# Fifth modulation vector taken out of the attention heads and put ahead of them; all modulation vectors on four column groups of 32

## What is computed

```python
m = silu(cvec) @ w_mod[l] + b_mod[l]               # 1024 x 6144, for c_ctx and for c
sh1, sc1, g1, sh2, sc2, g2 = m.reshape(6, 1024)
h = rms_norm(x, n1) * (1 + sc1) + sh1
q, k, v, u = split(h @ w_in)                       # 8 query heads, 2 KV heads of 64; u is 2 x 512
attn = attention(norm_rope(q), norm_rope(k), v)    # latent tokens also see 128 cached keys
conv = silu(layer_norm(depthwise_conv31(glu(u))))
x = x + g1 * (concat(attn, conv) @ w_out)
h2 = rms_norm(x, n2) * (1 + sc2) + sh2
x = x + g2 * moe(h2)                               # 16 experts, best group of 4, top 2 in it
```

## Time and profile before

| | us |
|---|---|
| median of 3 runs | 1130.35 |
| the runs | 1130.08, 1130.35, 1140.29 |
| the profiled execution, its own time | 1134.84 |
| its span from first to last instruction | 1133.0 |
| PE busy in it | 1003.9 (89%) |
| DVE busy | 393.6 (35%) |
| ACT busy | 152.3 (13%) |
| POOL busy | 116.3 (10%) |

### The profile page before, as it was taken

How to read it: one execution, slowest core, us unless ns; L and a number is a source line. 1 busy time by engine, 2 the same in 40 slices (tenths; PEclk the granted TensorE clock), 3 DMA queues, 4 the chain that set the end, 5 groups by cost and what they waited for, 6 DMA issues and landing times. The chain is left out here.

```text
span 1133.0 us, 11425 instructions
## 1 busy us (share of the span) xinstructions
PE 1003.9 (89%) x4328; PEld 471.3 (42%) x4328; DVE 393.6 (35%) x857; ACT 152.3 (13%) x357; POOL 116.3 (10%) x176
## 2 busy tenths in 40 slices
PE   4799999999799998899899989999788888987993
PEld 1555544545233333333366534555433333333331
DVE  0159954334411111111035996434511111111106
ACT  1100144220000000000020014422000000000001
POOL 0100400501000000000111020050100000000001
PEclk9899989998899999999899999999689899999897
DMA  9926991259999996999980375235966999999814
GB/s 341 354 117 238 291 366 70 95 189 360 419 404 423 425 372 273 413 422 424 360 306 24 149 277 215 75 115 195 371 237 240 417 422 425 424 423 422 353 28 167
DMA packets 64406, 329.83 MB, mean 291 GB/s; under 512 B 6992, under 2 KB 9680, under 8 KB 47924
## 3 DMA queue, kind: packets, MB, share of 16 engines
q1 hardware_dynamic: 44224, 277.89, 61.2%
q0 software_dynamic: 8496, 28.68, 6.9%
q10 hardware_dynamic: 11588, 21.95, 5.9%
HBM read 306.67 MB, written 21.82 MB: 290 GB/s over the span
## 5 line engine op out<-in xcount | busy, mean ns | idle before, releaser
L1746 PE MATMUL ps<-big 128*64 128x512 f32 x1024 | 245.5, 631 | 29.0 <-DMA big<-in_w_up_dram 11.8
L1762 PE MATMUL ps<-big,scr 128*64 128x512 f32 x624 | 151.0, 623 | 5.3 <-DVE scr L1399 4.3
L1441 PE MATMUL ps<-big 128*128 128x384 f32 (+2 forms) x448 | 147.9, 492 | 5.2 <-ACT big L777 5.2
L1746 PEld LDWEIGHTS ps<-big 128*64 128x64 f32 x1024 | 81.7, 145 | 168.1 <-issue 157.1
L1102 DVE SCALAR_TENSOR_TENSOR scr<-scr,convw 128x384 f32<-128x384 f32 x240 | 134.0, 611 | 2.3
L1410 DVE TENSOR_TENSOR scr<-ps,scr 128x256 f32<-128x256 f32 x32 | 13.6, 425 | 315.5 <-ACT scr L932 315.5
L1441 PEld LDWEIGHTS ps<-big 128*128 128x128 f32 x448 | 86.0, 193 | 64.7 <-issue 24.6
L1457 PE MATMUL ps<-big,cs_rep 128*64 128x512 f32 x320 | 80.8, 656 | 14.0 <-DMA big<-in_w_mod_dram 14.0
L1762 PEld LDWEIGHTS ps<-big,scr 128*64 128x64 f32 x624 | 51.2, 143 | 91.1 <-issue 89.0
L1662 PE MATMUL ps<-big 128*128 128x512 f32 x192 | 84.4, 594 | 1.4 <-ACT big L817 1.4
L1746 PE MATMUL ps<-big,scr 128*64 128x512 f32 x224 | 51.3, 612 | 5.9 <-DVE scr L1388 5.9
(11 more groups left out here) (220 smaller groups left out, 819.7 us busy)
## 6 DMA issues: line engine op xcount, KB each, us to landing
big<-in_w_gate_dram SPq DMA_DIRECT2D x32, 2048.0 KB, 15.8
big<-in_w_up_dram SPq DMA_DIRECT2D x32, 2048.0 KB, 19.7
big<-in_w_down_dram SPq DMA_DIRECT2D x32, 2048.0 KB, 16.7
big<-in_w_mod_dram SPq DMA_DIRECT2D x23, 2048.0 KB, 15.5
big<-in_w_in_dram SPq DMA_DIRECT2D x6, 2048.0 KB, 26.8
expert_rows<-scr ACTq DMA_DIRECT2D x74, 128.0 KB, 8.2
big<-in_w_out_dram SPq DMA_DIRECT2D x4, 2048.0 KB, 15.6
expert_rows<-x ACTq DMA_DIRECT2D x1, 6912.0 KB, 42.0
```

Source lines behind the costliest of these rows:

```text
L1441: mm = pe.matmul(out, stationary(k), moving(k), start=(k == 0), stop=(k == n - 1))
L1746: mm = pe.matmul(ps[b * TT:(b + 1) * TT, bank, :].rearrange("p (m n) -> p m n", m=2), tokens(k), w[:, :, k, b * HF:(b + 1) * HF], start=(k ...
L1762: mm = pe.matmul(ps[b * TT:(b + 1) * TT, bank, :], src[:, k % 2 * P + k // 2 * TT:k % 2 * P + (k // 2 + 1) * TT], w[:, k, b * SEG:(b + 1) ...
```

## The change

All vectors, the fifth too, are computed on four lanes of 256 outputs, on column groups of 32: a k-step is four matmuls of 256 columns (eight records), `columns` has 32 matmuls for 16, `lane_in` and `lane_out` issue four DMAs for two. `head_fill` is gone. Vector 4 runs as a whole on PE after the third tile's transposes and the end of vector 3, ahead of the scores of head 0, into PSUM bank 2; DVE takes it right after vector 3, ahead of `score_max` of head 0, in two instructions of 256 columns each, and the transposes of head 0 wait for that take. Its bias and the norm weight come in by `lane_in` (four DMAs each for one), together with vector 3's; its store is four DMAs for one.

```diff
-LANES = 2
+LANES = 4
-TAKES = [0, 1, 2, 3, 8, 9, 5]
+TAKES = [0, 1, 2, 3, 4, 5]
-    return {3: 0, 8: 0, 9: 0, 5: 3}[j]
+    return {3: 0, 4: 2, 5: 3}[j]
-HEAD_FILL = [(8 + hd // 4, hd % 4 * (KD // 4), (hd % 4 + 1) * (KD // 4)) for hd in range(HEADS)]
...
                 lane_in(pool, rowB, b_mod[l:l + 1, 3 * D:4 * D], rowB_in)
-                pool.dma_start(rowS, b_mod[l:l + 1, 4 * D:5 * D].broadcast_to([2, D])).then_inc(rowB_in, 16)
+                lane_in(pool, rowS, b_mod[l:l + 1, 4 * D:5 * D], rowB_in)
+                lane_in(pool, gainB, norm2_g[l:l + 1, :], rowB_in)
...
-                pool.wait_ge(slot_used[slot_of(("in", l, 3))], uses(("in", l, 3)))
-                pool.dma_start(gainB, norm2_g[l:l + 1, :].broadcast_to([2, D])).then_inc(gain_in, 16)
                 pool.wait_ge(mod_done, l + 1)
                 lane_out(pool, mod_dram[:, 3 * D:4 * D], rowB, modB_st)
-                pool.dma_start(mod_dram[:, 4 * D:5 * D], rowS).then_inc(modB_st, 16)
+                lane_out(pool, mod_dram[:, 4 * D:5 * D], rowS, modB_st)
...
-                    v.tensor_copy(rowA[:, c * LW:(c + 1) * LW], ps[:, bank, :]).then_inc(mod_taken, 1)
+                    v.tensor_copy(rowA[:, c * LW:(c + 1) * LW], ps[:, bank, 0:LW]).then_inc(mod_taken, 1)
...
+                row = (rowC, rowB, rowS, rowG)[c - 2]
+                v.tensor_tensor(row, ps[:, bank, 0:LW], row, ALU.add).then_inc(mod_taken, 1)
+                if c == 4:
                     dve.wait_ge(mod_taken, taken_at(l, c))
+                    v.scalar_tensor_tensor(row, row, 1.0, gainB, ALU.add, ALU.mult).then_inc(mod_done, 1)
...
                 mod_take(l, 3)
+                mod_take(l, 4)
...
-                    if HEAD_FILL[hd][2] == KD:
-                        mod_take(l, HEAD_FILL[hd][0])
...
-                            mm = pe.matmul(ps[lane * LP:(lane + 1) * LP, mod_bank(l, j), :], cs_rep[:, k, :],
+                            mm = pe.matmul(ps[lane * LP:(lane + 1) * LP, mod_bank(l, j), 0:LW], cs_rep[:, k, :],
                                            w[:, lane * LW:(lane + 1) * LW], start=(k == 0), stop=(k == KD - 1))
...
+                vector(l, 4)
                 pe.wait_ge(qkT_ready, l * 4 + 4)
                 for t in range(TILES):
                     scores(0, t)
...
                         if hd == 0 and t == 0:
-                            pe.wait_ge(mod_taken, taken_at(l, 3))
+                            pe.wait_ge(mod_taken, taken_at(l, 4))
...
-                    head_fill(l, hd)
...
-                    if n == 0:
-                        pe.wait_ge(mod_taken, taken_at(l, 9))
```

More of the change, by code:

```diff
@@ L288, in build @@
         zT = cut(CM * CONV_W).rearrange("p (m n) -> p m n", m=CM)
-        assert o >= 5120 + 3 * LW
+        assert o >= 6656
         qk_sq = scr[:, TILES * 640 + 2 * 640:2 * TILES * 640 + 2 * 640].rearrange("p (t n) -> p t n", t=TILES)
@@ L293, in build @@
         ck = cut(KVW)
-        sg = rowC = cut(CH)
+        sg = cut(CH)
+        rowC = sg[:, 0:LW]
         assert o <= 9832
@@ L308, in build @@
         colA = scr[:, 7168 + 2 * LW:7168 + 2 * LW + 3 * KD].rearrange("p (s k) -> p s k", k=KD)
-        rowB, rowS, rowG = scaleB[:, 0, 0:LW], shiftB[0:2, 0], scr[:, 6656:6656 + LW]
+        rowB, rowS, rowG = scaleB[:, 0, 0:LW], shiftB[:, 0, 0:LW], scr[:, 6656:6656 + LW]
         diag = h[:, :, 0:P]
-        gainB = hT[0][0:2].rearrange("p k n -> p (k n)")
+        gainB = shiftB[:, 0, LW:2 * LW]
         def lane_in(eng, rows, vec, done):
@@ L361, in build @@
         x_in = sem("x_in"); table_in = sem("table_in"); c_in = sem("c_in"); router_in = sem("router_in")
-        rowB_in = sem("rowB_in"); gain_in = sem("gain_in"); small_in = sem("small_in")
+        rowB_in = sem("rowB_in"); small_in = sem("small_in")
         modB_st = sem("modB_st"); modG_st = sem("modG_st"); rowC_in = sem("rowC_in")
@@ L374, in build @@
         out_st = sem("out_st")
-        mod_half_ps = sem("mod_half_ps")
         convw_ps = sem("convw_ps"); hT_ps = sem("hT_ps"); proj_ps = sem("proj_ps"); conv_ps = sem("conv_ps")
@@ L597, in _ @@
                 lane_out(pool, mod_dram[:, 2 * D:3 * D], rowC, modC_st)
-                pool.wait_ge(modC_st, (l + 1) * 32)
+                pool.wait_ge(modC_st, (l + 1) * LANES * 16)
                 spread(gateB[:, :, :], 2, bcG_in)
-                pool.wait_ge(slot_used[slot_of(("in", l, 3))], uses(("in", l, 3)))
-                pool.dma_start(gainB, norm2_g[l:l + 1, :].broadcast_to([2, D])).then_inc(gain_in, 16)
                 pool.wait_ge(mod_done, l + 1)
                 lane_out(pool, mod_dram[:, 3 * D:4 * D], rowB, modB_st)
-                pool.dma_start(mod_dram[:, 4 * D:5 * D], rowS).then_inc(modB_st, 16)
+                lane_out(pool, mod_dram[:, 4 * D:5 * D], rowS, modB_st)
                 pool.wait_ge(cache_st, l * 32 + 32)
@@ L628, in _ @@
                 ln_silu(2)
-                pool.wait_ge(modB_st, l * 48 + 48)
+                pool.wait_ge(modB_st, (l + 1) * 2 * LANES * 16)
                 spread(scaleB[:, :, :], 4, bcA_in)
@@ L653, in _ @@
                 lane_out(pool, mod_dram[:, 5 * D:6 * D], rowG, modG_st)
-                pool.wait_ge(modG_st, (l + 1) * 32)
+                pool.wait_ge(modG_st, (l + 1) * LANES * 16)
                 spread(gateB[:, :, :], 5, bcG_in)
@@ L963, in mod_take @@
                 if c == 2:
-                    dve.wait_ge(rowC_in, (l + 1) * 32)
+                    dve.wait_ge(rowC_in, (l + 1) * LANES * 16)
                 if c == 3:
-                    dve.wait_ge(rowB_in, (l + 1) * 48)
+                    dve.wait_ge(rowB_in, (l + 1) * 3 * LANES * 16)
                 if c == 5:
[L968 to L973, removed]
+                    dve.wait_ge(rowG_in, (l + 1) * LANES * 16)
+                n = pieces(l, c)[-1][0]
+                dve.wait_ge(slot_used[slot_of(n)], uses(n))
                 if c < 2:
-                    v.tensor_copy(rowA[:, c * LW:(c + 1) * LW], ps[:, bank, :]).then_inc(mod_taken, 1)
+                    v.tensor_copy(rowA[:, c * LW:(c + 1) * LW], ps[:, bank, 0:LW]).then_inc(mod_taken, 1)
                     return
[L977 to L986, removed]
+                row = (rowC, rowB, rowS, rowG)[c - 2]
+                v.tensor_tensor(row, ps[:, bank, 0:LW], row, ALU.add).then_inc(mod_taken, 1)
+                if c == 4:
                     dve.wait_ge(mod_taken, taken_at(l, c))
-                    ins = v.scalar_tensor_tensor(row, row, 1.0, gain, ALU.add, ALU.mult)
-                    if c != 8:
-                        ins.then_inc(mod_done, 1)
+                    v.scalar_tensor_tensor(row, row, 1.0, gainB, ALU.add, ALU.mult).then_inc(mod_done, 1)
             def columns(l):
```

## The result

The changed kernel takes 1158.85 us (median of 4 runs, 1155.33 to 1164.42) beside 1130.72 for the kernel before: a ratio of 1.024, 95% interval 1.0204 to 1.0277. It is slower, by about 28 us, where 29 us less was forecast. The profiled execution took 1164.42 us, its span 1162.6.

A forecast was written before the change was run, and what follows sets the result against it. PE was taken to bound the heads, DVE layer 0's conv taps, DMA part of layer 1's experts; -2.6 + 1.1 - 11.2 - 4.8 + 2.0 - 11.0 - 2.4 = -28.9 us gave a median of 1101.5, range 1092 to 1118.

The forecast's parts named there:

- Eight heads lose 1.81 us each: 14.5 us a layer, 6.68 down to 4.87 a head: Heads of both layers: PE sets their time, so removing the four fill records saves 14.5 us a layer.
- the heads run cold: Rival, chance 0.07: without the fill, the heads of transposes, scores and short products run at a low granted clock.
- against: Argument against cold heads: between fills PE does 4.87 us of this work, and layer 1's heads were at 1.00 throughout.
- The start: Layer 0, vector 1 behind `x_transposed`: -3.3 us, its copy on DVE -0.3, its columns +1.0, net -2.6.
- Four lanes: Vectors on PE: a k-step takes 0.47 us instead of 0.88, so 3.8 us a vector for 7.0.
- the rival that only two groups run side by side: Rival, chance 0.15: a vector's k-step on PE stays at 0.88 us, for -7.9 us in all, 1122.5.
- Vector 4 in the open: Ahead of the heads, nothing covers vector 4 on PE: +3.1 in layer 0 (DVE +3.3), +3.5 in layer 1.
- the third rival: Chance 0.08: vector 4's load holds the heads of layer 0, up to 10 us late, some 1108 us.
- POOL's queue: Bias loads and row stores go from 15 to 36 DMAs a layer; only layer 0's vector 2 load is uncovered, +1.1 us.
- Vector 5 and the way in: From vector 5 to the experts: -4.8 us in layer 0 (bounds -2.4 and -6.5), -2.4 in layer 1.
- Columns of layer 1: Between two experts on PE: 64 records, +4.0 us at today's pitch, 0 at half of it, +2.0 taken.
- An earlier end of the heads therefore moves the experts as a whole: Expert loads begin as the first experts free their slots, so earlier heads shift the experts; earlier loads alone gain 0.

The follow-up runs named there:

- lanes only: Kernel before with four lanes for vectors 0, 1, 2, 3 and 5, vector 4 left in the heads as their fill: 1131.19 us, ratio 0.9989.
- the two kernels with a step a head: Changed kernel with vector 4 dealt into the heads, one k-step each, on four lanes (1163.12 us) or two, other vectors on four (1183.08 us).
- two lanes ahead: Changed kernel with two lanes instead of four, vector 4 still ahead of the heads: 1170.01 us, ratio 1.0342 to the kernel before.

## Why the prediction was wrong

The step that failed is "Eight heads lose 1.81 us each: 14.5 us a layer, 6.68 down to 4.87 a head". It took the fill out of the head and left the clock at 1.00. The rival *the heads run cold*, at 0.07, is what happened: 8.92 us a head at 0.50 where the forecast had 4.87 at 1.00, and 1158.85 us in all. The heads at 4.87 us exist, in six kernels above; the change doesn't reach them.

The wrong turn is in the rival's "against". That layer 1's heads did this work at 1.00 between two fills shows that it holds the clock for as long as a head lasts without its fill (4.87 us), and the runs agree (seven such heads in a row at 1.00, with the fill in head 0 alone). It doesn't say what raises a clock that has fallen, and the rows that did were quoted beside it: head 0 of layer 0 was at 0.50 after a wait of 1.18 us, and head 1 was at 1.00 (160 to 164 us), with only the fill of 3.57 us and the products with v between. PE's timeline of the kernel before, the end of head 0 and the fill of head 1:

```profile
157.79 2.17 PE L1441 MATMUL ps<-scr 128*128 128x64 f32 x14
...
163.06 1.88 PE L1471 MATMUL ps<-big,cs_rep 128*2 128x512 f32 x4
```

The fill had a second job, and the edit that removes it also keeps a wait ahead of the first head. The right question was what, after the change, wakes PE after its last wait.

What is shown and what isn't: that PE is awake behind two idle matmuls (3.07 us, then heads at 1.00) and that it stays awake over a filled wait (1.00 from head 0 on) is shown. That the length of the wait alone decides is not so. Of the 28 head stages in these traces (14 kernels, two layers) the six whose wait was filled were awake from the first head; of the other 22 only layer 1 before was, after 1.19 us, while 1.18 in its layer 0 and 0.79 in layer 1 with lanes only were followed by a fall to 0.50. In three stages of the 22 (layer 0 of lanes only and of the two kernels with a step a head) there was no wait left at head 0 at all: PE came cold from the wait for `rope` (4.81 to 5.34 us), ran the scores cold (3.35 us) and went on so. Why waits of 1.18 and 1.19 us ended differently is not shown by any run.

The other steps, in the order of the sum:

- *The start* was too small: -6.4 us at the first conv matmul (54.8 to 48.39), -2.6 forecast. Vector 1 halved as forecast (3.66 for 7.09); its `columns` were to cost 1.0 more and cost 0.9 less (1.17 us for 64 records, 2.09 for 32 before). From the start of `x_transposed` that makes 4.6 (26.8 us before, 22.2 after). The other 1.8 lie ahead of it and are not shown to be the lanes': with two lanes ahead it began at 24.0 us, after at 26.2, before at 28.0.
- *Four lanes* were right: ten steps in 4.52 us, 0.45 a step (forecast 0.47; the ten took 8.80 before), so the rival that only two groups run side by side falls.
- *Vector 4 in the open* was right, and its row (137.45) shows no wait for a load, the third rival: from the first conv matmul to head 0 the gain of 6.4 fell to 3.3, so 3.1 us, +3.3 forecast for it, and +2.5 for layer 1 up to the scores.
- *POOL's queue*, +1.1: it doesn't show; the 3.1 us between the same two points leave no room for it.
- *Vector 5 and the way in*: -4.9 for -4.8 in layer 0, with the counts right behind the routing (278.82, a wait of 0.36 for DVE); -1.4 for -2.4 in layer 1.
- *Columns of layer 1*: -1.8 us for +2.0 (2.17 us, 4.01 before). A record with 32 columns to load took 17 to 18 ns, not the half of 63 that was the lower bound.
- *"An earlier end of the heads therefore moves the experts as a whole"* held only within some us. From the first expert's start to layer 1's first record on PE it was 264.4 us before, 272.2 after, and from 259.0 to 269.6 in the twelve others; layer 1's, to the end of PE's last record, 295.6, 292.5, and 290.5 to 297.1. PE's groups in layer 0's experts (busy, mean ns, idle before by releaser), first of the kernel before, then of the one after:

```profile
L1746 PE MATMUL ps<-big 128*64 128x512 f32 x512 | 121.3, 622 | 13.5 <-issue 7.6 <-DVE big L1379 5.8
...
L1778 PE MATMUL ps<-table_sb 128*1 128x1 f32 x70 | 4.4, 163 | 0.0
```

```profile
L1708 PE MATMUL ps<-big 128*64 128x512 f32 x512 | 121.4, 627 | 16.1 <-issue 9.0 <-DMA big<-in_w_up_dram 4.1 <-DVE big L1360 2.9
...
L1740 PE MATMUL ps<-table_sb 128*1 128x1 f32 x70 | 4.4, 164 | 3.8 <-issue 3.8
```

  The busy times of these groups agree; what has grown is mostly the time in which PE waits for nothing that the profile shows ("issue", 7.6 to 12.8 us in these rows) and a wait for the load of an up matrix (4.1 us, none before in this stretch). Why these differ between kernels with the same experts was not tried and stays open; it took part of the gain of the lanes alone.

## What to carry to other kernels

Before an instruction is taken out of a PE-bound loop, ask whether it is what brings the clock back after the last wait: look at the granted clock of the loop's first pass, of the wait ahead of it, and of what stands between the first slow and the first fast pass. That the loop's other work was seen at 1.00 said here that it could hold that clock (4.87 us a head behind one fill), not that it could raise it (8.92 us a head, at 0.50 in all of them from the second on, without one). If a filler must go, put the work that it did, or idle matmuls, into the wait ahead of the loop: here the change with vector 4 ahead of the scores cost 28 us, and with it behind them saved 42.

## What the runs showed that was not expected

- The same heads have two steady paces, 4.87 and 8.92 us, and PE counts as busy all the time in both; adding one fill to head 0 of each layer (3.07 us in layer 0) turned one into the other and made the kernel 44 us faster (1158.85 to 1114.8).
- A wait of 0.79 us was once enough to be followed by 0.50, and one of 1.19 us once was not.
- One idle matmul a head didn't raise the clock: it took 1.87 us cold, as long as two awake (1.88), and made the kernel 18 us slower than none (1177.23 for 1158.85).
- On column groups of 32, records with two moving columns followed each other every 17 to 18 ns (64 in 1.17 us, 128 in 2.17), against 63 on groups of 64.
